# Feed-forward gate and up products with the weights stationary instead of the tokens, without the turning of the gated values

## What is computed

```python
FFN_HIDDEN = -(-8 * D_MODEL // (3 * 256)) * 256        # 2816
...
    h2 = rms_norm(x, ffn_norm_gain)
    gate, up = jnp.split(jnp.einsum('bsd,df->bsf', h2, w_gate_up), 2, axis=-1)
    return x + jnp.einsum('bsf,fd->bsd', jax.nn.silu(gate) * up, w_down)
```

## Time and profile before

| | us |
|---|---|
| median of 3 runs | 1236.47 |
| lowest, highest | 1230.64, 1238.16 |
| the profiled execution, its span | 1235.8 |
| PE busy | 1084.6 |
| PE weight loads busy | 596.4 |
| VectorE busy | 383.6 |
| ScalarE busy | 264.1 |

### The profile page before, as it was taken

One profiled execution on the slowest core, in us unless ns is written; L12 is line 12 of the kernel. 1 busy time (PEld: TensorE's weight loads), 2 busy tenths in 40 slices (PEclk: granted clock), 3 DMA queues, 4 the chain that ended last, 5 costly groups with the idle time before them and its releaser, 6 DMA issues.

```text
span 1235.8 us, 15026 instructions
## 1 busy us (share of the span) xinstructions
PE 1084.6 (88%) x6106; PEld 596.4 (48%) x6106; DVE 383.6 (31%) x1032; ACT 264.1 (21%) x429; POOL 2.9 (0%) x9
## 2 busy tenths in 40 slices
PE   6999988988899999999999987898777787888874
PEld 5845458765454444444457644443333443344332
DVE  2140566553340000000121756542233222223222
ACT  0105312332110000000121201342232222233220
POOL 0000000000000000000000000000000000000000
PEclk9999989989989999999999997999989989899898
DMA  9444231011311342523900453899999999999992
GB/s 384 177 150 159 113 136 69 1 60 48 122 69 68 139 167 102 202 104 138 381 25 1 166 224 155 342 429 427 430 426 430 427 430 427 430 427 430 427 429 101
DMA packets 24218, 289.58 MB, mean 234 GB/s; under 512 B 2775, under 2 KB 4280, under 8 KB 6392
## 3 DMA queue, kind: packets, MB, share of 16 engines
q1 hardware_dynamic: 24184, 289.08, 56.9%
HBM read 288.03 MB, written 1.05 MB: 234 GB/s over the span
## 4 chain that ended last, share of the span: by engine, by line
PE 59%; DMA 26%; DVE 11%; issue 2%; ACT 2%; SPq 1%; DVEq 0%
DMA sb_ring<-w_exp 25%; PE ps L917 12%; PE ps L594 7%; PE ps L934 6%; PE ps L342 5%; PE ps L614 4%; PE ps L987 3%; PE ps L864 2%; PE ps L833 2%; PE ps L366 2%; PE ps L997 1%; PE ps L973 1%; PE ps L959 1%; DVE sb_own L1508 1%; PE ps L358 1%
## 5 line engine op out<-in xcount | busy, mean ns | idle before, releaser
L342 PE MATMUL ps<-sb_ring,sb_own 128*32 128x256 f32 x1984 | 138.8, 441 | 77.2 <-DMA sb_ring<-w_exp 76.5
L917 PE MATMUL ps<-sb_ring,sb_hT 128*128 128x512 f32 x352 | 155.2, 600 | 0.9 <-DVE sb_hT L1440 0.9
L342 PEld LDWEIGHTS ps<-sb_ring,sb_own 128*32 128x32 f32 x1984 | 82.3, 126 | 145.4 <-issue 123.5
L366 PE MATMUL ps<-sb_own 128*128 128x512 f32 x256 | 115.2, 593 | 0.9 <-DVE sb_own L1936 0.9
L917 PEld LDWEIGHTS ps<-sb_ring,sb_hT 128*128 128x128 f32 x352 | 67.8, 193 | 86.3 <-issue 86.3
L594 PE MATMUL ps<-sb_ring,sb_hT 128*128 128x512 f32 (+1 forms) x256 | 104.7, 570 | 0.5 <-DVE sb_small L1479 0.5
L934 PE MATMUL ps<-sb_ring,sb_gatedT 128*128 128x512 f32 x176 | 78.2, 597 | 8.6 <-ACT sb_gatedT L1326 8.6
L1727 DVE TENSOR_TENSOR sb_nsa<-sb_nsa,ps 128x256 f32<-128x256 f32 x22 | 8.4, 418 | 222.5 <-ACT sb_nsa L1324 222.5
L594 PEld LDWEIGHTS ps<-sb_ring,sb_hT 128*128 128x128 f32 x256 | 48.5, 190 | 54.4 <-issue 52.1
L1918 DVE TENSOR_TENSOR sb_own<-sb_own,ps 128x128 f32<-128x128 f32 x32 | 9.2, 289 | 199.2 <-ACT sb_own L1390 199.1
L366 PEld LDWEIGHTS ps<-sb_own 128*128 128x128 f32 x256 | 46.2, 190 | 47.7 <-issue 47.7
(11 more groups left out here) (395 smaller groups left out, 1237.4 us busy)
## 6 DMA issues: line engine op xcount, KB each, us to landing
sb_ring<-w_exp SPq DMA_DIRECT2D x94, 2048.0 KB, 21.4
sb_ring<-w_in SPq DMA_DIRECT2D x14, 2048.0 KB, 11.3
sb_ring<-w_gu SPq DMA_DIRECT2D x11, 2048.0 KB, 9.1
sb_ring<-w_dn SPq DMA_DIRECT2D x11, 1024.0 KB, 4.9
sb_ring<-w_out SPq DMA_DIRECT2D x4, 2048.0 KB, 8.6
sb_ring<-w_branch SPq DMA_DIRECT2D x2, 2048.0 KB, 8.1
sb_ring<-cmp_w SPq DMA_DIRECT2D x1, 2048.0 KB, 8.1
sb_nsa<-w_exp SPq DMA_DIRECT2D x1, 1280.0 KB, 9.5
```

The lines of the kernel that those rows point to most:

```text
L342: m = pe.matmul(ps[group(j), 2, 0:256], hgT[:, k, :], w[j // 2][k][:, (j % 2) * 256:(j % 2 + 1) * 256], start=(k == 0), stop=(k == KT - 1))
L366: m = pe.matmul(ps[:, 4 + 2 * b + half, :], pickT[par][:, b, :], down_part[:, half * BANK:(half + 1) * BANK], start=start, stop=stop, skip ...
L917: m = pe.matmul(ps[:, 2 * s.par + b, :], hT[:, k, b * P:(b + 1) * P], w[:, k, :], start=(k == 0), stop=(k == KT - 1))
```

## The change

`gate_up` swaps the operands. Four times eight matmuls: for each of four groups c of 128 hidden values (two of gate, two of up) a 128x128 piece of weights is stationary and the 256 tokens of `hT` move. The result has hidden values on partitions and tokens as columns; gate fills bank 2 par, up fills bank 2 par + 1, and gu_made is incremented once behind gate and once behind up. ScalarE applies Silu to the gate bank in one 128x512 instruction, straight into `gatedT`, whose layout is now hidden group by token; it waits for the gate products and, from step 2 on, for the down product that read that parity of `gatedT` before. VectorE multiplies `gatedT` in place by the up bank in one 128x512 instruction and increments gatedT_ready. The transposes, the signals gated_ready and gated_turned, the tile view `gated` and ScalarE's copy are gone. ScalarE's loop has one turn less and single steps around it. Two more lines only rename the axes of flat views of `gatedT`. SyncE's program is not touched, nor are the weights' layouts in memory.

```diff
@@ -222,8 +222,7 @@
         job_heads = lambda flat, half: flat.rearrange("p (g r d) -> p g r d", g=NSA_G, r=NSA_R)[:, :, 2 * half:2 * half + 2, :]
 
 
-        gated = nsa.rearrange("p b h d -> p (b h d)")[:, 0:1024].rearrange("p (i b n) -> p i b n", i=2, b=NB)
-        gatedT = ctx.enter_context(nc.sbuf_tensor("sb_gatedT", [P, 2, NB, FC // P, P], F32))[:]
+        gatedT = ctx.enter_context(nc.sbuf_tensor("sb_gatedT", [P, 2, FC // P, T], F32))[:]
...
@@ -907,31 +906,27 @@
             def gate_up(s, first=False):
 
                 pe.wait_ge(sig(f"gu{s.par}_loaded"), 16 * s.turns)
-                w = ring[:, s.par, :].rearrange("p (k n) -> p k n", n=BANK)
-                if not first:
+                w = ring[:, s.par, :].rearrange("p (k c n) -> p k c n", c=4, n=P)
+                if first:
+                    pe.wait_ge(sig("h2_ready"), since("h2_ready", 4))
+                else:
                     pe.wait_ge(sig("gatedT_ready"), s.n - 1)
-                for b in range(NB):
-                    if first:
-                        pe.wait_ge(sig("h2_ready"), since("h2_ready", 4))
+                for c in range(4):
                     for k in range(KT):
-                        m = pe.matmul(ps[:, 2 * s.par + b, :], hT[:, k, b * P:(b + 1) * P], w[:, k, :],
+                        m = pe.matmul(ps[:, 2 * s.par + c // 2, (c % 2) * T:(c % 2 + 1) * T], w[:, k, c, :], hT[:, k, :],
                                       start=(k == 0), stop=(k == KT - 1))
-                    m.then_inc(sig("gu_made"), 1)
+                    if c % 2:
+                        m.then_inc(sig("gu_made"), 1)
 
             def down(s, start=False, stop=False):
 
-                pe.wait_ge(sig("gated_ready"), s.n + 1)
-                for b in range(NB):
-                    for f in range(FC // P):
-                        m = pe.transpose(ps[:, 2 * s.par + b, f * P:(f + 1) * P], gated[:, s.par, b, f * P:(f + 1) * P], ident)
-                m.then_inc(sig("gated_turned"), 1)
                 pe.wait_ge(sig(f"dn{s.par}_loaded"), 16 * s.turns)
                 pe.wait_ge(sig("gatedT_ready"), s.n + 1)
                 w = ring[:, 2, s.par * 2048:(s.par + 1) * 2048].rearrange("p (f n) -> p f n", n=D)
                 for b in range(NB):
                     for half in range(2):
                         for f in range(FC // P):
-                            m = pe.matmul(ps[:, 4 + 2 * b + half, :], gatedT[:, s.par, b, f, :], w[:, f, half * BANK:(half + 1) * BANK],
+                            m = pe.matmul(ps[:, 4 + 2 * b + half, :], gatedT[:, s.par, f, b * P:(b + 1) * P], w[:, f, half * BANK:(half + 1) * BANK],
                                           start=start and f == 0, stop=stop and f == FC // P - 1, skip_group_check=True)
                 m.then_inc(sig("down_made"), 1)
...
@@ -1318,18 +1313,20 @@
             act.activation(kern_abs.rearrange("p d b n -> p (d b n)"), kern.rearrange("p d b n -> p (d b n)"), ACT.Abs).then_inc(sig("kern_abs_ready"), 1)
             root(stat[:, 0:NB], "row_mean", 2, "row_root")
 
-            def ffn(s):
-                for b in range(NB):
-                    act.wait_ge(sig("gu_made"), 2 * s.n + b + 1)
-                    act.activation(gated[:, s.par, b, :], ps[:, 2 * s.par + b, 0:FC], ACT.Silu).then_inc(sig("gate_ready"), 1)
-                act.wait_ge(sig("gated_turned"), s.n + 1)
-                act.activation(gatedT[:, s.par].rearrange("p b f n -> p b (f n)"), ps[:, 2 * s.par:2 * s.par + 2, 0:FC], ACT.Copy)\
-                   .then_inc(sig("gatedT_ready"), 1)
-
-            ffn(Step(0))
-            with act.Fori(0, (N_FC - 1) // 2) as i:
+            def ffn(s, first=False):
+                act.wait_ge(sig("gu_made"), 2 * s.n + 1)
+                if not first:
+                    act.wait_ge(sig("down_made"), s.n - 1)
+                act.activation(gatedT[:, s.par].rearrange("p f t -> p (f t)"), ps[:, 2 * s.par, :], ACT.Silu).then_inc(sig("gate_ready"), 1)
+
+            ffn(Step(0), first=True)
+            ffn(Step(1), first=True)
+            with act.Fori(0, (N_FC - 3) // 2) as i:
                 for parity in range(2):
-                    ffn(Step(i=i, parity=parity))
+                    s = Step(i=i, parity=parity)
+                    s.n, s.par = 2 * i + parity + 2, parity
+                    ffn(s)
+            ffn(Step(N_FC - 1))
...
@@ -1722,10 +1719,10 @@
             turned_out(0, "x2_turned", "h2_ready", C_FFN)
 
             def ffn(s):
-                for b in range(NB):
-                    dve.wait_ge(sig("gate_ready"), 2 * s.n + b + 1)
-                    ins = dve.tensor_tensor(gated[:, s.par, b, :], gated[:, s.par, b, :], ps[:, 2 * s.par + b, FC:2 * FC], ALU.mult)
-                ins.then_inc(sig("gated_ready"), 1)
+                dve.wait_ge(sig("gate_ready"), s.n + 1)
+                dve.wait_ge(sig("gu_made"), 2 * s.n + 2)
+                mine = gatedT[:, s.par].rearrange("p f t -> p (f t)")
+                dve.tensor_tensor(mine, mine, ps[:, 2 * s.par + 1, :], ALU.mult).then_inc(sig("gatedT_ready"), 1)
 
             ffn(Step(0))
             with dve.Fori(0, (N_FC - 1) // 2) as i:
```

More of the change, by code:

```diff
@@ L244, in two_layer_program @@
         nsa_flat = nsa.rearrange("p b h d -> p (b h d)")
-        gatedT_flat = gatedT.rearrange("p i b f n -> p (i b f n)")
+        gatedT_flat = gatedT.rearrange("p i f t -> p (i f t)")
         emb, filt_in, filt_mid = gatedT_flat[0:33, 768:1024], small[0:33, 128:192], small[0:64, 192:320]
@@ L261, in two_layer_program @@
         prodF = hT.rearrange("p k t -> p (k t)").rearrange("p (f n) -> p f n", n=DH2)
-        cross = gatedT.rearrange("p i b f n -> p (i b f n)").rearrange("p (f n) -> p f n", n=DH2)
+        cross = gatedT.rearrange("p i f t -> p (i f t)").rearrange("p (f n) -> p f n", n=DH2)
         y_hy = own[:, 1, :].rearrange("p (c t) -> p c t", t=T)
```

## The result

| | before | after |
|---|---|---|
| median, us | 1235.11 (4 runs) | 1216.63 (4 runs) |
| lowest, highest | 1230.64, 1238.16 | 1213.47, 1219.37 |
| profiled span | 1235.8 | 1214.1 |

The ratio is 0.9842, 95% interval 0.9804 to 0.9880: 18 to 20 us faster, where 12.4 had been forecast and 1218 was the lower end of the range. Two later comparisons of the same two kernels gave 0.9885 (0.9847 to 0.9924) and 0.9840 (0.9798 to 0.9882), with medians of 1219.4 and 1218.7 us for the changed kernel. The mean of the three ratios is 0.9856, 17.8 us of 1236.

A forecast was written before the change was run, and what follows sets the result against it. TensorE was taken to bound the feed-forward stage and DMA the expert stage. Removing 13.3 us and adding 0.9 gave 12.4 us less, all passed on: 1224 us from a median of 1236.47, range 1218 to 1232.

The forecast's parts named there:

- what is removed: Feed-forward stage: transposes, ScalarE's copy and the waits around it leave TensorE's path, 1.21 us in each of 11 steps, 13.3 us.
- Exchanged, 0.9 us: Gate and up: 32 matmuls of 256 columns replace 16 of 512, costing 0.08 to 0.09 us per step, 0.9 in 11.
- Margin of the loads, 26 ns: Gate and up: a weight load of 190 ns still fits under a 256-column pass of 216 ns, a thin margin.
- Rival 3: Gate and up: weight loads come out from under the passes; wholly exposed 134 us more, about 1358 us; chance 5%.
- The new wait costs nothing: Down's wait for VectorE's gatedT_ready is covered by the product between; without that cover 0.9 us per step, 10 in all.
- The clock: these 2.65 us stay: First two gate-and-up products: half clock makes them 30.11 instead of 27.46 us, and the change leaves these 2.65 us.
- Do the weights keep up: Feed-forward stage: a gate-and-up weight tile lands in 9.1 us, with 12 us of slack before and 11 after the change.
- Is it passed on: Behind the stage: the expert weight stream's releases all come earlier, so the kernel's end moves by the whole 12.4 us.
- if its length stays: Expert stage: the saturated weight stream, released 12.4 us sooner, ends 12.4 us sooner provided its length is unchanged.
- The range: Whole kernel: 1218 to 1232 us, taking in the 256-column form at a slower pace; the forecast's own range was 1220 to 1228.
- The line at 1%: Whole kernel: 1% of 1236.47 is 12.4 us, exactly the sum, splitting the forecast's 80% into 44 faster and 36 within 1%.

The follow-up runs named there:

- turn_hidden: Kernel before, with the transposes of one step moved between the two token blocks of the next step's gate and up; ratio 0.9936 to the kernel before.
- own_down: Changed kernel with each down product right behind its own gate and up, so nothing covers VectorE's product; ratio 0.9999 to the kernel before.
- tokens256: Kernel before, tokens still stationary, with each 512-column gate-and-up matmul made as two of 256; 1236.0 us in one run.
- n64: Changed kernel with 64 instead of 256 tokens per gate-and-up matmul, 256 passes per step; 1441.8 us.
- shift2: Changed kernel with two 512-wide matmuls of constants behind the last down product, delaying what follows by 1.72 us; 1218.1 us in one run.
- shift3: Changed kernel with three 512-wide matmuls of constants behind the last down product, delaying what follows by 2.57 us; 1223.4 us in one run.
- n128: Changed kernel with 128 instead of 256 tokens per gate-and-up matmul, 128 passes per step; 1226.4 us, ratio 0.9949 to the kernel before.

## Why the prediction was wrong

**Wrong by size.** The direction and the mechanism were right, the amount was not: 12.4 us forecast, 18.5 between the medians, 17.8 by the mean of three comparisons. The step that failed is the term "what is removed": it left out 0.24 us per step. The steps one by one:

- *Removed, 11 x 1.21 = 13.3 us.* The term was mis-sized. The sum took "down 7.10" from the earlier trace rows as the price of the product, when 0.24 of it belonged to the wait in front. The rows ahead of the prediction had what was needed: 32 passes of L917 take 13.73 us, so 16 of the same width take 6.87. A step's loss was 1.45 us, 16.0 in 11 steps; turn_hidden took 0.24 away with the wait, own_down brought it back with the wait. That adds 2.6 us to the gain.
- *Exchanged, 0.9 us.* Right: 13.81 per step, as in L987's row. tokens256 shows that it is the width.
- *Margin of the loads, 26 ns.* Wrong, without effect on the sum. It compared a pass with the length of a load's row; loads follow each other in 0.111 us (n64). Rival 3, loads that come out from under the passes, was further away than its 5% said.
- *The new wait costs nothing.* Right. own_down shows 8.9 us of waiting where nothing covers it, and with the 0.24 us behind each wait 21.73 - 20.68 = 1.05 us per step, where the prediction had 0.9.
- *The clock: these 2.65 us stay.* Half right: 2.25 us of them were gone in the first profile and back in the next two. The step overlooked that half-clock stretches elsewhere move too: the output product of the second mixer became 1.7 us shorter, in all three profiles of the changed kernel, and was as long as before again when the work behind the stage was delayed (shift2, shift3). No step of the sum looked at what a shift of 12 to 15 us does to half-clock stretches behind it; that term stood at nothing without a reason.
- *Do the weights keep up.* Right. The gate-and-up tile still lands in 9.1 us and no wait of PE names it.
- *Is it passed on.* Right for the stage's gain. Behind the stage the program takes 622.9 and 623.5 us in before and 620.4, 621.7 and 621.7 in after: nothing is lost there, and those 1.7 us show on top within the spread. The condition "if its length stays" was too simple: from the start of the first piece of expert transfer in the chain to the end, before takes 1235.8 - 830.65 = 405.2 us and after 1214.1 - 812.31 = 401.8.

```profile
812.31 22.96 DMA sb_ring<-w_exp
```

By the traces the change gives -16.0 + 0.9 = 15.1 us less. (The rest of the stage shows 15.3, since only nine of the eleven narrower products lie in it.) With the 1.7 us behind the stage it is 16.8 us, a ratio of 0.9864, inside all three intervals. The mean ratio says 17.8; the 1.0 between is under what these runs resolve.

The first two profiles differ by 21.7 us. Of these 15.3 lie in the rest of the stage, 2.25 in the first two products, 1.7 in the first projection (43.44 against 41.68 us, code that is not changed) and 2.5 behind the stage. The last are 1.7 in the output product, 1.7 in the last expert's product (5.38 against 3.69) and 1.7 in the twelve rounds of the expert stage before it, less 2.6 between the output product and the first expert transfer, where after takes 84.4 us and before 81.8.

**The range.** 1218 to 1232 took its lower end from the spread of runs around a sum that was 2.6 us short, and held no case of a further gain. With the mis-sized term put right the sum gives 1236.5 - 15.1 = 1221.4, inside the range; the 1.7 us of the output product and 3 us more, which no trace assigns and which are about what the changed kernel's own medians differ by, lead to the measured 1216.6. The two later medians, 1219.4 and 1218.7, lie inside the range. The line at 1% that had seemed to cut the forecast in two lay 3 us from the 15.1.

## What to carry to other kernels

The price of a wait is not the idle time alone: compare the product behind it with one of the same passes that stands in a row without a gap, and add the difference (0.24 us here, 11 times). Take the pace of a matmul shape from how many passes fill how many us, never from the length of its load rows. And split two profiles at the ends of the changed stage before reading a difference: here the unchanged part in front of it differed by up to 14 us.

## What the runs showed of the hardware

- Weight loads of 128 columns follow each other every 0.111 us at full clock (n64) though the rows are 190 ns long (n128, after). A pass of 128 columns takes 0.112, of 256 0.216, of 512 0.429; at 64 columns it is 0.111 still.
- In n64 PE was busy 40.00 of 40.00 us at a granted clock of 0.50 (400 to 440), and it stayed at half clock for over 100 us, through 512 passes of 64 columns (109.46 us, 0.214 each). It rose in the down product that followed, 16 passes of 512 columns in 9.14 us instead of 6.92, and stayed up through the later steps of 256 narrow passes. With 128 columns the same place was cold for some us only (31.14 us for 256 passes instead of 28.6). Why the clock stayed down there and what raised it was not tried further.
- A product behind a wait costs 0.24 us more than the same product in a row. The timeline shows the first load of down and its first pass, in before and in after:

```profile
465.11 0.30 PEld L934 LDWEIGHTS ps<-sb_ring,sb_gatedT 128*128 128x128 f32 x2 [0.99 <-issue]
465.14 1.10 PE L934 MATMUL ps<-sb_ring,sb_gatedT 128*128 128x512 f32 x2 [0.78 <-ACT sb_gatedT L1326]
```

```profile
434.79 0.41 PEld L929 LDWEIGHTS ps<-sb_ring,sb_gatedT 128*128 128x128 f32 x2
435.01 2.31 PE L929 MATMUL ps<-sb_ring,sb_gatedT 128*128 128x512 f32 x5
```

In after the load starts 0.22 us ahead of the pass, under the passes before it; in before only 0.03 us, behind the wait. That it is this load which is laid open is read from these two places and not tested by itself.
